# The forget gate's weights: from an early load of their own to a chunk in the weight ring

## The reference, cut to what matters

```python
h = _rmsnorm(x, attn_norm[layer])                      # 512 x 1024
proj = h @ w_in[layer]                                 # 1024 x 3080
qa, ka, va, qf, kf, vf, f_pre = jnp.split(proj, splits, axis=-1)   # six of 512 columns, f_pre has 8
...
log_f = jax.nn.log_sigmoid((f_pre + b_forget[layer]).astype(jnp.float32))
# forgetting attention: c = cumsum(log_f), logit[t, s] += c[t] - c[s]
```

## Time and profile before

| | |
|---|---|
| median of three runs | 2092.59 us |
| the profiled execution | 2092.59 us, its span 2090.7 us |
| TensorE busy | 1879.5 us, 90% of the span |
| VectorE, ScalarE, GpSimd busy | 764.9, 582.1, 171.4 us |
| granted TensorE clock, mean | 0.922 |
| moved by DMA | 261.19 MB, mean 125 GB/s |
| `p_2` | its matmuls begin at 1407.67 us, the last evacuation is at 1553.94 us |

### The profile page before, as it was taken

One profiled execution on the slowest core, in us unless ns is written; L12 is line 12 of the kernel. 1 busy time (PEld: TensorE's weight loads), 2 busy tenths in 40 slices (PEclk: granted clock), 3 DMA queues, 4 the chain that ended last, 5 costly groups with the idle time before them and its releaser, 6 DMA issues. The chain is left out here.

```text
span 2090.7 us, 21944 instructions
## 1 busy us (share of the span) xinstructions
PE 1879.5 (90%) x9058; PEld 1413.7 (68%) x9058; DVE 764.9 (37%) x1146; ACT 582.1 (28%) x888; POOL 171.4 (8%) x216
## 2 busy tenths in 40 slices
PE   4997999999989957999799999979999985999992
PEld 3875888878768847778588887868777774333330
DVE  3235222223353442553422223352336444222323
ACT  4225222222342141352522222252235410000001
POOL 4000000000000010010000000000000201242422
PEclk9978999999989975699799999989999885999996
DMA  6212233333213321801233332223230043899983
GB/s 166 98 36 76 81 100 90 90 101 101 89 54 100 84 64 35 260 1 46 56 100 92 89 100 101 91 91 101 81 121 21 7 166 151 337 389 382 387 328 133
DMA packets 182319, 261.19 MB, mean 125 GB/s; under 512 B 19064, under 2 KB 139032, under 8 KB 169696
## 3 DMA queue, kind: packets, MB, share of 16 engines
q1 hardware_dynamic: 158880, 204.66, 29.7%
q0 software_dynamic: 19328, 26.06, 4.0%
q10 hardware_dynamic: 4032, 29.36, 3.6%
HBM read 297.82 MB, written 29.40 MB: 157 GB/s over the span
## 5 line engine op out<-in xcount | busy, mean ns | idle before, releaser
L147 DVE TENSOR_TENSOR RING_R<-RING,RING_R 128x2048 fp32r<-128x2048 f32 (+1 forms) x110 | 249.9, 2274 | 758.2 <-ACT RING_R L144 758.2
L166 PE MATMUL PB<-RING_R,OPS_R 128*128 128x512 f32 (+1 forms) x1056 | 412.5, 391 | 14.8 <-issue 6.0
L167 PE MATMUL PB<-RING_R,OPS_R 128*128 128x512 f32 (+1 forms) x1056 | 410.6, 389 | 0.0
L168 PE MATMUL PB<-RING_R,OPS_R 128*128 128x512 f32 (+1 forms) x1056 | 410.6, 389 | 0.0
L144 ACT ACTIVATE RING_R<-RING 128x2048 fp32r<-128x2048 f32 (+1 forms) x110 | 208.6, 1898 | 465.3 <-DMA RING<-in_ffn_w_down 139.3
L166 PE MATMUL PB<-OPS_R,RING_R 128*128 128x512 f32 x704 | 275.9, 392 | 5.5 <-DVE OPS_R L289 5.5
L167 PE MATMUL PB<-OPS_R,RING_R 128*128 128x512 f32 x704 | 275.4, 391 | 0.0
L168 PE MATMUL PB<-OPS_R,RING_R 128*128 128x512 f32 x704 | 275.1, 391 | 0.0
L166 PEld LDWEIGHTS PB<-RING_R,OPS_R 128*128 128x128 f32 x1056 | 200.4, 190 | 57.4 <-issue 13.6
L167 PEld LDWEIGHTS PB<-RING_R,OPS_R 128*128 128x128 f32 x1056 | 200.3, 190 | 40.2
L168 PEld LDWEIGHTS PB<-RING_R,OPS_R 128*128 128x128 f32 x1056 | 199.9, 189 | 40.6
(11 more groups left out here) (342 smaller groups left out, 2002.0 us busy)
## 6 DMA issues: line engine op xcount, KB each, us to landing
RING<-in_ffn_w_gate SPq DMA_DIRECT2D x44, 512.0 KB, 3.9
RING<-in_ffn_w_up SPq DMA_DIRECT2D x44, 512.0 KB, 5.2
RING<-in_ffn_w_down SPq DMA_DIRECT2D x44, 512.0 KB, 4.2
RING<-in_w_expert_gate SPq DMA_DIRECT2D x16, 1024.0 KB
RING<-in_w_expert_up SPq DMA_DIRECT2D x16, 1024.0 KB
OPS<-in_w_expert_gate SPq DMA_DIRECT2D x16, 1024.0 KB
OPS<-in_w_expert_up SPq DMA_DIRECT2D x16, 1024.0 KB
Y<-in_w_expert_down ACTq DMA_DIRECT2D x14, 1024.0 KB
```

Source lines behind the costliest of these rows:

```text
L147: nc.vector.tensor_tensor(RING_R[:, raw], RING[:, raw], RING_R[:, high].bitcast(fp32), ALU.subtract).then_inc(s_wlo, 1)
L166: nc.tensor.matmul(o, x[0], w[0], start=start, stop=False)
L167: nc.tensor.matmul(o, x[0], w[1], start=False, stop=False)
L168: return nc.tensor.matmul(o, x[1], w[0], start=False, stop=stop)
```

## The change

The 8 columns are no longer loaded by GpSimd into ST. They become a chunk of their own in the ring, 64 words a partition, added between the chunks (3, 0) and (3, 1) of `p_2` by a new argument `extra` of `Proj`. Its "done" is `g_mm`, the end of the forget product. Its split is done by `split_to`, as for all chunks, so the two split functions and the semaphore `g_w` go, and so does the second view of ST. `s_2` counts two loads instead of three.

```diff
@@ -88,10 +88,7 @@
         X = sb("X", [P, MT, D])
         Y = sb("Y", [P, MT, D])
         Z = sb("Z", [P, MT * OD])
-        ST_AT = -(-nc.sbuf_base // 32) * 32
-        sb("st_area", [P, 2112])
-        ST = nc.alloc_sbuf_tensor_at("ST", [P, 2112], fp32, offset=ST_AT)
-        ST_R = nc.alloc_sbuf_tensor_at("ST_R", [P, 2112], fp32r, offset=ST_AT)
+        ST = sb("ST", [P, 2112])
...
-            def __init__(self, name, norm, w, width, dst, fn, paired=None, order=None, banks=8):
+            def __init__(self, name, norm, w, width, dst, fn, paired=None, order=None, banks=8, extra=None):
...
@@ -323,6 +320,8 @@
                 for j, (c0, c1) in enumerate(self.cols):
                     wd = c1 - c0
                     for hf in range(2):
+                        if extra and (j, hf) in extra:
+                            extra[j, hf]()
                         n = self.index[j, hf] = len(chunks)
                         dst_ = ring_slot(n)[:, 0:4 * wd].rearrange("p (k n) -> p k n", k=4)
...
-        g_w = sem("forget_weights_split")
-        fp_raw = ST[:, 2048:2048 + KT * NH]
-        fp_h, fp_l = ST_R[:, 0:KT * NH], ST_R[:, 2048:2048 + KT * NH]
-
-        p_2 = Proj("in2", n5, a["w_in_2"][0], FP_, Z2, alt, order=[1, 0, 2, 4, 3, 5], banks=4)
-
-        def forget_split_act():
-            nc.scalar.wait_ge(s_2, 16 * 3)
-            nc.scalar.wait_ge(b_dr, 16)
-            nc.scalar.activation(fp_h, fp_raw, ACT.Copy).then_inc(g_w, 1)
-
-        def forget_split_dve():
-            nc.vector.wait_ge(g_w, 1)
-            nc.vector.tensor_tensor(fp_l, fp_raw, fp_h.bitcast(fp32), ALU.subtract).then_inc(g_w, 1)
+        fp_chunk = []
+
+        def forget_chunk():
+            n = len(chunks)
+            w_v = a["w_in_2"][0].rearrange("(k p) n -> p k n", p=P)
+            dst_ = ring_slot(n)[:, 0:KT * NH].rearrange("p (k n) -> p k n", k=KT)
+            add_chunk(*((dst_[:, 4 * h:4 * h + 4], w_v[:, 4 * h:4 * h + 4, FP_:FP_ + NH]) for h in range(2)), words=KT * NH)
+            chunks[n]["done"] = (g_mm, 1)
+            fp_chunk.append(n)
+
+        p_2 = Proj("in2", n5, a["w_in_2"][0], FP_, Z2, alt, order=[1, 0, 2, 4, 3, 5], banks=4, extra={(3, 1): forget_chunk})
 
         def forget_pe(pe):
-            pe.wait_ge(g_w, 2)
+            wait_split(pe, fp_chunk[0])
             turned_wait(pe, 2)
-            wh, wl = [x.rearrange("p (k n) -> p k n", k=KT) for x in (fp_h, fp_l)]
+            wh, wl = [x.rearrange("p (k n) -> p k n", k=KT) for x in parts(fp_chunk[0])]
             for k in range(KT):
                 t = product(PB[0:NH, 0, :], (wh[:, k], wl[:, k]), (HTH[:, k, :], HTL[:, k, :]), start=(k == 0), stop=(k == KT - 1))
             t.then_inc(g_mm, 1)
...
         def forget_dve():
             dve = nc.vector
-            dve.wait_ge(s_2, 16 * 3)
+            dve.wait_ge(s_2, 16 * 2)
...
         def bias_pe(pe):
-            pe.wait_ge(s_2, 16 * 3)
+            pe.wait_ge(s_2, 16 * 2)
...
-            for dst, src in ((bfr[:], a["b_forget_2"].rearrange("a h -> h a")), (rb[:], a["rel_bias_2"]),
-                             (ST[:, 2048:2048 + KT * NH].rearrange("p (k n) -> p k n", k=KT),
-                              a["w_in_2"][0].rearrange("(k p) n -> p k n", p=P)[:, :, FP_:FP_ + NH])):
+            for dst, src in ((bfr[:], a["b_forget_2"].rearrange("a h -> h a")), (rb[:], a["rel_bias_2"])):
                 pool.dma_start(dst, src, allow_slow_non_contiguous=True).then_inc(s_2, 16)
...
-            p_2.take(act, "act", {0: forget_split_act, 3: forget_act}, {1: turn_take(0), 2: turn_take(1), 4: turn_take(2), 5: turn_take(3)})
+            p_2.take(act, "act", {3: forget_act}, {1: turn_take(0), 2: turn_take(1), 4: turn_take(2), 5: turn_take(3)})
...
-            p_2.take(dve, "dve", {0: forget_split_dve, 3: forget_dve}, {1: turn_take(0), 2: turn_take(1), 4: turn_take(2), 5: turn_take(3)})
+            p_2.take(dve, "dve", {3: forget_dve}, {1: turn_take(0), 2: turn_take(1), 4: turn_take(2), 5: turn_take(3)})
```

## The result

| | before | after |
|---|---|---|
| median of five runs | 2092.59 us | 2106.08 us |
| lowest to highest | 2084.96 to 2097.99 us | 2102.89 to 2109.19 us |
| ratio, 95% interval | | 1.0075 (1.005 to 1.0098) |
| the profiled execution's span | 2090.7 us | 2101.4 us |

A forecast was written before the change was run, and what follows sets the result against it. The prediction took TensorE, busy 90% of the span, to bound the kernel. A wait of 11.87 us plus 1.6 of slower clock made 13.5, so 2092.6 + 13.5 = 2106.1 us, range 2098 to 2112.

The forecast's parts named there:

- What bounds the kernel: Whole kernel: TensorE is busy 90% of the span of 2090.7 us, so only its time counts.
- The wait before (3,0): In `p_2`: evacuations of group 2 stand behind the split of late-loaded (3,1); TensorE idles 11.3 us, +11.87 us.
- The load's duration: Load of (3,1) in `p_2`: 5.38 us from issue to start of split, with 5.20 to 6.91 as ends.
- The clock behind it: In `p_2` after the idle time before (3,0): TensorE at half speed for 3.2 to 3.6 us, +1.6 us.
- The wait before (4,0): In `p_2`: (4,1) loads later by the forget matmuls, but its split is 0.6 us ahead of need; cost 0.
- T: The time at which TensorE ends chunk (3,0) of `p_2`, forecast at 1502.33 us.
- Rival 1: In `p_2`: another 1.0 us at (4,0) and up to 2.0 for the small pieces; 2109 to 2111 us, chance 0.15.
- The small load: The 1024 pieces of 32 bytes, now on SyncE's queue before (3,1): covered by 12.65 us, cost 0.
- Downstream: After `p_2`: nothing holds the shift back, since later loads are each issued on a semaphore of the work before.
- Rival 2: Expert stage: its end is set by its transfers, so the shift vanishes there; 2092.6 us, chance 0.06.
- Rival 3: At 797 to 811 and 819 to 835 us: clock stays at 1.00, up to 14.5 us back; 2091.6 us, chance 0.04.

The follow-up runs named there:

- evac_first_g2: Changed kernel, but in column group 2 of `p_2` the tiles are turned and evacuated before chunk (3,1) is split; 2092.12 us, ratio 1.0014 to the kernel before.
- dummy_in2: Kernel before, with an unused chunk of 64 words added to the ring between (3,0) and (3,1) of `p_2`; 2105.14 us, ratio 1.0081.
- half_late: Changed kernel, but in column group 2 of `p_2` the split of (3,1) comes between the second and third evacuation; 2096.76 us, ratio 1.0033 to the kernel before.
- dummy_od: Kernel before, with an unused 64-word chunk between (1,0) and (1,1) of `p_od`, a projection with eight banks; 2090.81 us, ratio 1.0003.
- early_load_later: Kernel before, with GpSimd's early load of the forget weights issued after the first output projection; 2093.0 us, ratio 1.0008.

## Why the prediction was right

*What bounds the kernel*, TensorE with everything behind it in its shadow, held: the time lost in `p_2` is TensorE's idle time, 11.4 us, and its slower matmuls, 2.3.

*The wait before (3,0).* Each step has its row. Issue to split 1486.18-1480.87 = 5.31 (forecast 5.38); ScalarE's split to VectorE's 1.94 (1.95); to the turned tiles 2.22 (2.20); to the evacuation 1.19 (1.20); to the first matmul 0.83 (0.83). The gap is 11.52. The prediction gives 11.3 in words, but its own steps, 5.38 and 6.18, add up to 11.56, and it is this that the sum uses and the trace bears out. `evac_first_g2` shows that the wait needs the order, and `dummy_in2` that it needs the place in the ring and no other part of the change. That it also needs the four banks is seen in `half_late`, where TensorE got as far as the freed banks let it, and agrees with `dummy_od`, which is another projection.

*The load's duration* was within 0.1 us of the row of before. The fit of the Trainium skill (DMA: Bandwidth & Descriptors, section "Anatomy of one DMA — SWDGE (gpsimd) path") would have given an estimate of 4.4 us for 1 MB. It is stated for one DMA from GpSimd; this load, two DMAs of 512 KB on SyncE's queue, took 5.3 from its issue to its split.

*The clock behind it* is the term that was mis-sized. I took 3.2 us at half speed, a loss of 1.6, from a place with an idle time of 6.74 us. After this one it lasted 4.8 and 5.2 us in the two profiles and 4.5 in `dummy_in2` (1490.57 to 1495.0). From its first matmul to its end (3,0) took 1505.80-1492.36 = 13.44 us, 1504.57-1490.94 = 13.63 and 1503.85-1490.57 = 13.28, where (1,0) behind its short wait took 11.19: the clock cost 2.3, 2.4 and 2.1 us. The term was short by 0.5 to 0.8 us of a sum of 13.5, and above the upper end I gave it, 1.8. From the end of (2,1) to the end of (3,0) the sum gives 13.5 more than before, and the first profile has 24.93-10.88 = 14.05. The way through `p_2` came out 13.7 and 14.3 longer, not 13.5; that the medians gave 13.5 to the tenth is luck, with an interval of 10.5 to 20.5 us on the first comparison.

*The wait before (4,0)*, forecast at 0 with 0.6 us of slack: none. (4,1) was issued at T + 5.54 (1511.34-1505.80, forecast 5.5) and the end of (3,1) is at T + 16.42. Rival 1 is out.

*The small load*: issued at 1468.22, its split began at 1470.98, 2.8 us later. The 13.8 us of the earlier trace rows did not belong to its small pieces, nor to GpSimd's queue: `early_load_later` issued the same load on the same queue at 197.1 us, and it landed after 3.6. The DMA engines were 95% busy in the first 36 us (25% from 195 to 202 in `early_load_later`), so it may have waited for them; no run separates this from what else differed there. The rule of the Trainium skill that a transfer under 512 B falls under line rate (DMA: Bandwidth & Descriptors, section "Specifications") may hold for it, which no run here shows; at 2.8 us of the 12.65 there was nothing to pay.

*Downstream* the change itself gave nothing back: the attention's first two waits are the same as before, 0.69 and 1.23 us, and in the second profile the shift stays at 14.1 us up to the expert stage and the span is 14.0 longer. The first profile's span from `p_2`'s end on did get 4.7 us shorter, by the clock of that run. Rival 2 is out. *Rival 3* wanted the clock freed in the second layer. The stretches by stage of the changed kernel's profile (columns as above):

```profile
797.00:811.00 14.00, 12.06 (x57) 11.88 (x56) 0.33 (x2) 0.00 (x0) 0.00 (x0) 0.50 0.05 17
819.00:835.00 16.00, 16.00 (x90) 15.07 (x90) 1.69 (x5) 0.24 (x2) 0.00 (x0) 0.50 0.13 42
```

Both stand at 0.50, as before. The clock was not freed, and rival 3 is out.

## What to carry to other kernels

When a ring or a queue gets one more entry, write out for each entry behind it which older one it now waits for, and then what stands behind its first consumer in an ordered queue: the cost is not the late load, but the finished work queued behind the wait for it. Evacuations that free scarce banks belong ahead of a wait for data that is needed only later. At the end of this projection the same move put a split ahead of the attention's first work and cost 3.3 us, so each place has to be looked at. The two profiles of one kernel here differ by 3.3 us in span, mostly by the clock granted behind `p_2`, so a change of this size is read from the stretch it touches, not from the spans.

## What was not expected of the hardware

How long the lower clock lasted behind an idle time was not one number: 2.9 us after a gap of 4.92, 4.5 to 5.2 after gaps of 11.5, always with the same 512-column matmuls behind it, and 3.2 after the 6.74 us of the earlier trace rows. Three gaps of the long kind and one of each shorter kind do not say whether the length follows from the gap or from chance, and that stays open. The clock fell even in the gap of 4.92 us.
